# One inference step of a hybrid decoder: state products that add in PSUM, and a shared transpose for the rotary keys

## The reference

```python
def one_seq(args):            # layer 0, one of 8 samples, against its 16 cached pages of 128 rows
    pt, qs, cn, krn = args
    c_all = jnp.concatenate([cache_c[m, pt].reshape(n_past, KV_RANK), cn], axis=0)        # 256 wide
    kr_all = jnp.concatenate([cache_kr[m, pt].reshape(n_past, ROPE_DIM), krn], axis=0)    # 64 wide
    k = mla_keys(c_all, kr_all, w_uk, g_kn)
    s = jnp.einsum('qhd,thd->hqt', qs, k) * ATTN_SCALE
    p = jax.nn.softmax(jnp.where(mask[None], s, -jnp.inf), axis=-1)
    o_lat = jnp.einsum('hqt,tr->qhr', p, c_all)
    return jnp.einsum('qhr,rhd->qhd', o_lat, w_uv)

def wkv_step(state, inp):     # layer 1, 16 heads with a state of 64x64, one token
    r, w, k, v, a, b = inp
    sa = jnp.einsum('bhij,bhj->bhi', state, a)
    state = state * w[:, :, None, :] + sa[..., None] * b[:, :, None, :] + v[..., None] * k[:, :, None, :]
    return state, jnp.einsum('bhij,bhj->bhi', state, r)
```

## Time and profile before

| | |
|---|---|
| median of 3 runs | 3057.46 us (3056.83 to 3058.86) |
| profiled execution, its own time | 3059.15 us |
| its span, first to last instruction | 3057.2 us |
| mean granted TensorE clock | 0.985 |
| busy: TensorE, VectorE, ScalarE, GpSimd | 95%, 69%, 44%, 23% of the span |
| the samples' stage | about 624 to 1175 us |
| the recurrence's chains | about 2286 to 2585 us |

### The profile page before, as it was taken

The page is one execution under the profiler, slowest core; times in us unless marked ns, Lnnn a source line. Parts: engine busy times, 40 slices in busy tenths (PEclk is TensorE's granted clock), DMA queues, the critical chain, the costliest instruction groups (busy, mean ns, idle before and its releaser), DMA issues.

```text
span 3057.2 us, 69119 instructions
## 1 busy us (share of the span) xinstructions
PE 2900.6 (95%) x28799; PEld 2779.1 (91%) x28799; DVE 2111.7 (69%) x2724; ACT 1349.4 (44%) x2410; POOL 714.0 (23%) x557
## 2 busy tenths in 40 slices
PE   8999999999999999999999999999878887999999
PEld 8999997589999988999999999999866776999999
DVE  6977865656666663788786977873446666488976
ACT  4433434445555552344344433433445554334432
POOL 1322210410000002123220322341035553211321
PEclk9999999999999999999999999999989999999999
DMA  3222212111111102232222223312100001222322
GB/s 118 96 98 87 93 65 75 29 45 36 36 36 49 51 34 69 70 97 91 89 83 81 94 89 97 97 56 83 63 3 19 19 19 42 83 79 87 95 85 87
DMA packets 78973, 208.21 MB, mean 68 GB/s; under 512 B 25505, under 2 KB 42274, under 8 KB 63714
## 3 DMA queue, kind: packets, MB, share of 16 engines
q1 hardware_dynamic: 78690, 204.16, 21.0%
HBM read 198.63 MB, written 5.49 MB: 67 GB/s over the span
## 4 chain that ended last, share of the span: by engine, by line
PE 85%; DVE 7%; ACT 4%; issue 3%; DMA 0%; POOL 0%; DVEq 0%; SPq 0%; POOLq 0%; ACTq 0%
PE PS L469 25%; PE PS L285 22%; PE PS L1589 11%; PE PS L2187 5%; PE PS L2479 5%; PE PS L642 5%; PE PS L1570 1%; PE PS L1616 1%; PE PS L2167 1%; DVE WL L269 1%; DVE DOWN L771 1%; DVE WL L435 1%; PE PS L1232 1%; PE PS L1213 1%; PE PS L1214 1%
## 5 line engine op out<-in xcount | busy, mean ns | idle before, releaser
L408 POOL TENSOR_TENSOR WLF<-RAW 128x512 f32<-128x512 f32 x72 | 94.0, 1305 | 979.2 <-PE PS L285 656.8
L264 ACT ACTIVATE WH<-RAW 128x1536 fp32r<-128x1536 f32 (+3 forms) x112 | 171.4, 1530 | 323.2 <-PE PS L285 195.6
L269 DVE TENSOR_TENSOR WL<-RAW,WH 128x1536 fp32r<-128x1536 f32 (+3 forms) x113 | 217.9, 1929 | 119.1 <-ACT WH L264 119.1
L1589 PE MATMUL PS<-UKMH,CTH 128*128 128x384 f32 (+1 forms) x768 | 269.3, 351 | 0.4 <-POOL RQL L1532 0.4
L469 PE MATMUL PS<-XH,WH 128*128 128x288 f32 x864 | 255.1, 295 | 8.3 <-DVE M L510 8.3
L1663 DVE TENSOR_REDUCE SS<-SQ 128x4 f32<-128x512 f32 x256 | 173.5, 685 | 119.9 <-ACT SQ L1648 118.0
L469 PE MATMUL PS<-XH,WL 128*128 128x288 f32 x864 | 255.2, 295 | 0.0
L469 PE MATMUL PS<-XL,WH 128*128 128x288 f32 x864 | 254.8, 295 | 0.0
L1589 PE MATMUL PS<-UKMH,CTL 128*128 128x384 f32 (+1 forms) x768 | 252.6, 329 | 0.0
L1648 ACT ACTIVATE SQ<-PS 128x384 f32<-128x384 f32 (+1 forms) x384 | 172.3, 455 | 132.5 <-PE PS L1589 132.5
L285 PE MATMUL PS<-HH,WH 128*128 128x288 f32 x1056 | 225.3, 295 | 1.2 <-DVE WL L269 1.2
(11 more groups left out here) (636 smaller groups left out, 9010.3 us busy)
## 6 DMA issues: line engine op xcount, KB each, us to landing
RAW<-in_w SPq DMA_DIRECT2D x113, 1024.0 KB, 4.9
RAW<-in_w SPq DMA_DIRECT2D x48, 768.0 KB, 5.0
ROWS<-in_cache_c SPq DMA_DIRECT2D x128, 128.0 KB, 2.0
RAW<-in_w SPq DMA_DIRECT2D x16, 512.0 KB, 4.4
ROWS<-in_cache_kr SPq DMA_DIRECT2D x128, 32.0 KB, 1.8
RAW<-in_w SPq DMA_DIRECT2D x8, 384.0 KB, 3.2
X<-in_x SPq DMA_DIRECT2D x4, 576.0 KB, 7.7
out_y<-X SPq DMA_DIRECT2D x8, 288.0 KB, 2.3
```

What stands on the lines that cost most here:

```text
L264: act.activation(WH[n % 2][:, 0:cols], RAW[n % 2][:, 0:cols], ACT.Copy).then_inc(rounded, 1)
L269: dve.tensor_tensor(WL[n % 2][:, 0:cols], RAW[n % 2][:, 0:cols], WH[n % 2][:, 0:cols].bitcast(F32), ALU.subtract).then_inc(item_split, 1)
L1589: mm = pe.matmul(out[:, 0:c1 - c0], c[u][:, x], w, start=t == 0, stop=t == 5)
```

## The change

It has two parts.

In the recurrence a state's product with GM is added in bank 4, where the chunk's part of GAM stands already. The copy of GAM by ScalarE goes, and so do the identity products. The two products of the samples' state move from bank 4 to bank 5, and the wait for `sfa` moves from the sums of KTOKP with vtok to the mean's product.

In the samples' stage the rotary rows get a buffer of their own, `KRS`, in which two neighbouring pages lie side by side. One transpose of 128x128 serves both: it is issued with the even page, and ScalarE copies the result with both. In even pages the rotary part lies in partitions 0 to 63, in odd pages in 64 to 127, and VectorE writes the remainder to the other half. `QL` gets the queries' remainder on partitions 0 to 63, where it had zeros, by a subtraction in place of a memset; TensorE waits for the first subtraction only, GpSimd for all three. The DMAs of the first sequence are issued as the space of each of the two buffers becomes free.

```diff
-    ROW = KV + 1 + ROPE
-    ROWS = m.at("ROWS0", A0 + 4032, [PAGES, ROW]), m.at("ROWS1", A0 + 13016, [PAGES, ROW])
+    ROW = KV + 1
+    KRS = m.at("KRS0", A0 + 4032, [PAGES, ROPE]), m.at("KRS1", A0 + 13016, [PAGES, ROPE])
+    ROWS = m.at("ROWS0", A0 + 5056, [PAGES, ROW]), m.at("ROWS1", A0 + 14040, [PAGES, ROW])
...
             sp.wait_ge(s_mm, 4 * h + 4)
-            ready = [p for p in range(PAGES) if min(((p + 1) * ROW - 1) // T, H - 1) == h]
-            rows_sp(sp, 0, pages=ready)
+            freed = lambda start, n: [p for p in range(PAGES) if min((start + (p + 1) * n - 1) // T, H - 1) == h]
+            rows_sp(sp, 0, pages=freed(PAGES * ROPE, ROW), rope=freed(0, ROPE))
...
-        pool.wait_ge(qz_split, 2)
+        pool.wait_ge(qz_split, 3)
...
-        for k, c in enumerate((0, P, ROW - P)):
-            mm = pe.transpose(bank(6)[:, k * P:(k + 1) * P], row[:, p, c:c + P], IDENT)
+        for k in range(KV_T):
+            mm = pe.transpose(bank(6)[:, k * P:(k + 1) * P], row[:, p, k * P:(k + 1) * P], IDENT)
+        if p % 2 == 0:
+            mm = pe.transpose(bank(6)[:, KV:KV + P], KRS[s % 2][:, p:p + 2, :].rearrange("p a r -> p (a r)"), IDENT)
         mm.then_inc(row_t, 1)
...
-        dve.tensor_tensor(CTH[u][0:ROPE, rope], bank(6, slice(ROPE, P))[:, rope], CTH[u][ROPE:P, rope].bitcast(F32), ALU.subtract).then_inc(row_lo, 1)
+        own = slice(u * ROPE, (u + 1) * ROPE)
+        other = slice(ROPE - u * ROPE, P - u * ROPE)
+        dve.tensor_tensor(CTH[u][other, rope], bank(6, own)[:, rope], CTH[u][own, rope].bitcast(F32), ALU.subtract).then_inc(row_lo, 1)
...
-        pe.wait_ge(qz_split, 2)
+        pe.wait_ge(qz_split, 1)
...
-        dve.memset(rope(QL)[0:64].bitcast(F32), 0.0).then_inc(qz_zero, 1)
...
-        dve.wait_ge(qz_zero, 1)
+        dve.wait_ge(qz_hi, 2)
+        dve.tensor_tensor(rope(QL)[0:64], QRS[0:64].rearrange("p s h q -> p (s h q)"), rope(QH)[0:64].bitcast(F32), ALU.subtract).then_inc(qz_split, 1)
...
                     wait("stc", NB * p + c)
-                    for r in HEADS:
-                        pe.matmul(cells(5)[r, c, :], GM[r, c, :], STC[r, c - 1, :], start=True, stop=False)
-                    for r in HEADS:
-                        mm = pe.matmul(cells(5)[r, c, :], EYE2[r, :], GAM[r, c, :], start=False, stop=True)
-                    mm.then_inc(q["st"], 1)
+                    sums(4, at(GM), lambda r, c: STC[r, c - 1, :], c, start=False, across=False).then_inc(q["st"], 1)
...
                 wait("gc", b)
-                wait("gamc", b)
...
-                    mm = pe.matmul(bank(4, r), KTOKS[r, p, :], flat(UVE)[r, :], start=True, stop=False)
+                    mm = pe.matmul(bank(5, r), KTOKS[r, p, :], flat(UVE)[r, :], start=True, stop=False)
...
-                    mm = pe.matmul(bank(4, r), BTOKS[r, p, :], flat(UVE)[r, :], start=False, stop=True)
+                    mm = pe.matmul(bank(5, r), BTOKS[r, p, :], flat(UVE)[r, :], start=False, stop=True)
...
                 wait("tkc", n)
-                if chain:
-                    wait("sfa", b)
...
             if chain:
+                wait("sfa", b)
                 wait("y_norm", y_at(b, "y_lo"))
...
-                    act.activation(STC[:, c, :], cells(5)[:, c, :], ACT.Copy, scale=pcl[:, c:c + 1]).then_inc(q["stc"], 1)
+                    act.activation(STC[:, c, :], cells(4)[:, c, :], ACT.Copy, scale=pcl[:, c:c + 1]).then_inc(q["stc"], 1)
...
-                act.activation(flat(GAM), bank(4), ACT.Copy).then_inc(q["gamc"], 1)
...
-                dve.tensor_tensor(flat(S0), flat(S0), bank(4), ALU.add).then_inc(q["sfa"], 1)
+                dve.tensor_tensor(flat(S0), flat(S0), bank(5), ALU.add).then_inc(q["sfa"], 1)
```

More of the change, by code:

```diff
@@ L1442, in program @@
     qz_hi = stage_sem("attention", "qz_hi")
-    qz_zero = stage_sem("attention", "qz_zero")
     qz_split = stage_sem("attention", "qz_split")
@@ L1488, in program, with rows_sp @@
     QUERY_COL = (0, 1088)
-    def rows_sp(sp, s, i=0, pages=range(PAGES)):
+    def rows_sp(sp, s, i=0, pages=range(PAGES), rope=range(PAGES)):
         u = s % 2
-        for p in pages:
+        for p in range(PAGES):
+            if p not in pages and p not in rope:
+                continue
             e = s * PAGES + p
@@ L1496, in rows_sp @@
             page = sp.value_load(at, min_val=0, max_val=POOL - 1)
-            sp.dma_start(ROWS[u][:, p:p + 1, 0:KV], a["cache_c"][bass.ds(page, 1), :, :].rearrange("o t r -> t o r")).then_inc(rows_in[u][p // 8], 16)
-            sp.dma_start(ROWS[u][:, p:p + 1, KV + 1:ROW], a["cache_kr"][bass.ds(page, 1), :, :].rearrange("o t r -> t o r")).then_inc(rows_in[u][p // 8], 16)
+            if p in pages:
+                sp.dma_start(ROWS[u][:, p:p + 1, 0:KV], a["cache_c"][bass.ds(page, 1), :, :].rearrange("o t r -> t o r")).then_inc(rows_in[u][p // 8], 16)
+            if p in rope:
+                sp.dma_start(KRS[u][:, p:p + 1, :], a["cache_kr"][bass.ds(page, 1), :, :].rearrange("o t r -> t o r")).then_inc(rows_in[u][p // 8], 16)
     def first_rows_sp(sp):
@@ L1540, in rope_pool @@
             pool.wait_ge(rows_in[u][half], 16 * PAGES * (s // 2 + 1) + 8 * PAGES * i)
-            kr = ROWS[u][:, half * 8:half * 8 + 8, KV + 1:ROW]
+            kr = KRS[u][:, half * 8:half * 8 + 8, :]
             pool.tensor_tensor(dst[:], kr, kr, ALU.mult).then_inc(rope_sq, 1)
@@ L2016, in program @@
     GM = blk("GM", 16)
-    GAM, YL = blk("GAM", 17), blk("YL", 17, F32R)
+    YL = blk("YL", 17, F32R)
     PT1, SQT_, XT = blk("PT1", 18), blk("SQT_", 18), blk("XT", 18)
```

## The result

The changed kernel takes **3042.14 us** (median of 4 runs, 3041.14 to 3043.62), the kernel before 3058.16 us in the runs beside it: a ratio of 0.995, with a 95% interval of 0.9938 to 0.9962, or 16 us less. The forecast was 3046.0 with a range of 3041 to 3052. The profiled execution has a span of 3041.8 us and a time of its own of 3043.62.

A forecast was written before the change was run, and what follows sets the result against it. TensorE was taken to bound both stages (busy 488 of 497 us in samples, 232 of 280 in the recurrence). Savings of 5.4 + 0.7 + 4.5 + 0.8 = 11.4 us from the median 3057.46 gave 3046.0, range 3041 to 3052.

The forecast's parts named there:

- The sum: Samples and recurrence: transposes 5.4, start 0.7, recurrence units 4.5 and last unit 0.8 make 11.4 us less.
- The chance of "faster": Whole kernel: chance of a measurement below 3051.3 us, given as 0.84.
- The transposes: Samples, odd pages: 49 of 64 removed transposes count, 0.11 us each, 5.4 us; most at pages 3 and 5 hide in waits.
- Page 4's wait 0.1 longer: Samples, sign of being right: TensorE's wait for VectorE at page 4 grows by 0.1 us.
- "more is kept" rival: Both stages: AR not late 2.8, fewer packets 1.4, pages 3 and 5 count 1.5 us; 3040.3 in all; chance 0.12.
- The start: Samples' start: query products wait for one correction step instead of two and start 0.7 us earlier.
- The copy: Recurrence, state 1: without ScalarE's GAM copy AR is late next, so 0.09 us a unit, 0.6 in all.
- state 1: Recurrence, a unit's first state: AR products start at 2451.91 instead of 2452.00, gaining 0.09 of the 0.49 us GAM wait.
- The products: Recurrence: identity products go, 0.12 us a state where not hidden; 0.55 us for each of seven units, 0.8 for the last.
- The last unit's states: Recurrence, last unit: states at 0.74 us instead of 0.86, each losing 0.12, 0.8 us together.
- Code: Recurrence, rival: unexplained waits are instruction fetch; takes its whole gain (3051.4) or adds 1.4 to 3.1 us; recurrence-gives-little chance 0.12.
- Slower by the clock: Recurrence, rival: clock falls to 1.2 GHz as TensorE waits 0.7 us for AR; 0.2% slower from some 35 us; chance 0.04.

The follow-up runs named there:

- the kernel with all transposes: Kernel after with the shared rotary transpose done again in every odd page (64 more transposes, result unchanged): 3051.11 us, ratio 0.9968 against before.
- samples only plus 16: Kernel before with only the samples' part of the change, plus 16 unused 64x64 products in a wait at the recurrence's start: 3053.04 us, ratio 0.9973.
- recurrence only: Kernel before with only the recurrence's part of the change, samples' stage as before: 3053.95 us, ratio 0.9979.
- after plus 16: Kernel after plus 16 unused 64x64 products (64 instructions) in a wait at the recurrence's start: 3045.50 us, ratio 0.9953 against before.
- samples only: Kernel before with only the samples' part of the change, recurrence as before: 3058.58 us, ratio 0.9991.
- after plus 48: Kernel after plus 48 unused 64x64 products (192 instructions) in a wait at the recurrence's start: 3054.95 us, ratio 0.9978 against before.

## Why the prediction was right, and where it was not

**The sum: right in total, by two errors that cancel.** The sum had 6.1 us for the samples and 5.3 for the recurrence. In the profiled executions the samples gave 7.7 (0.73 and 6.94), 1.6 us more, and the recurrence without the waits for code and the clock 3.5 (308.9 to 305.4, an estimate), 1.8 us less: 11.2 for the 11.4 forecast. The time came out 4 us under the forecast because 4.2 us of waits for code and some 0.9 of the lower clock were gained on top, for which the sum had nothing. (The chance of "faster" adds up to 0.83 by the halves named there, not 0.84.)

**The transposes: right, by its own steps.** 49 of 64 were to count, 5.4 us at 0.11. Measured 5.36 + 0.12 = 5.5 us, and the 14 at pages 3 and 5 lie inside VectorE's waits as the chain said. "Page 4's wait 0.1 longer" came out 0.06 shorter, since VectorE's CTL moved by 0.17 as well: 2.1 us at these pages that had no term, of which 1.5 are left over the stage (the 1.46 of the kernel with all transposes). The "more is kept" rival had 1.5 us at these pages for a wrong reason.

**The start: right.** 0.7 forecast, 0.73 measured.

**The copy: worth nothing, where 0.6 us were forecast.** The step said that the products with AR could follow VectorE's end by 0.05 us, as at the samples' start. They followed at 0.15 (2438.79 + 0.99 to 2439.93), as they had before (2451.85 to 2452.00), so state 1 gained 0 and not 0.09. That AR is late next and swallows the wait for GAM was right, and the kernel with the copy kept shows it.

**The products: right in kind, their size known only to some 2 us.** With the first place equal (0), the recurrence's part gave 6.0 us alone and 7.5 on top of the samples' part (3053.04 to 3045.50), where the sum had 5.3; but removing the products moves the waits inside the recurrence too. In the traces of before and after its work and its waits for other engines fell from 317.3 to 312.9 us, 4.4, of which 0.9 can be the clock. The column "rest" has 3.5 us between the means of three kernels with products and copy and nine without both, and 5.5 with the products put back, for the 4.7 of the forecast. The last unit's states stand at 0.75 us, forecast 0.74.

**Code: the rival was seen, but as the wrong thing.** The forecast treated the unexplained waits as something that either takes the gain or adds 1.4 to 3.1 us. The runs show that they follow the code's place against the packets, and that the place alone moves the kernel after by some 10 us with the work unchanged: 15.9 to 19.7 us less than before at place -64, 16.0 at 0, 12.4 at +64, 6.2 at +128. At one place the parts nearly add: -8.4 (samples only plus 16) and -6.0 (recurrence only) make -14.4, and after plus 16 has -16.0; at different places -1.4 and -6.0 make -7.4, 8.6 short of the whole. The whole change stands at a place as good as any tried, so its gain came out in full; with the code 192 instructions further on, the same change gave 6.2 us, the edge of what can be told from none. The forecast's value was in part luck in this term.

**Slower by the clock: too small a chance.** I gave 0.04 and held the 1.00 of the stretch against it. A fall within the recurrence exists, though not by the wait for AR that the rival named: in samples only the clock fell to 1.2 GHz three times (for 3.4, 3.4 and 6.8 us) where that of before did not, in after plus 48 twice (6.8 and 3.4), besides 10.2 us near the start where after has 3.4; each time behind waits for code. It did not fall in the kernel after between 2275 and 2555. That the waits cause the fall is argued from their order in time; no run set the waits without the code's place. And they don't decide it alone: samples only plus 16 has its waits where before has them, and its clock fell at 2464.8 and 2546.7, where that of before did not.

## What to carry to other kernels

In a stretch of many small TensorE instructions written out, a change of a few instructions anywhere ahead moves the waits for code, and here that was worth some 10 us of 3045, more than half of what the change itself gave. Judge such an edit with its place held fixed (pad with instructions in a wait until the packets stand as before), and count a stage that you did not touch as able to move. Where that can't be done, compare the stretch less its waits for code and less what the lower clock cost: that figure stood within 3 us over ten kernels whose recurrences differed by 18. A removed instruction inside a wait gives nothing, which the chain of releasers tells ahead; a removed wait is replaced by the next late input, and when that one lets TensorE go is read from its own row (0.15 us after VectorE's end here, not the 0.05 of another product).

## What was not expected of the hardware

- Waits with the releaser "issue" on TensorE repeat at the same product and to the hundredth of a us (1.18 and 1.18 and 1.18, 1.70 and 1.70) when the code's place is the same modulo 256 instructions, and stand elsewhere when it is not. 507 of 509 end 1.18 to 1.72 us after a packet of 16 KB of the instruction queue has landed.
- Adding 16 products to a kernel made it 5.5 us faster (3058.58 to 3053.04); adding 48 to another made it 9 to 13 us slower.
- VectorE's subtraction behind a long operation began 0.11 us earlier, and at one of two places ran 0.06 us shorter, in all twelve traces with the samples' part and in neither of the two without (0.88 for 0.99 us after the reciprocal's start, in seven of seven places each); its cause is open.
